# First recurrent head pair: its value projection spread over the parts of its triangular inverse, and its first factors made ahead of the last two receptance mixes

## The reference, cut to what matters

```python
Pm = Pf + (prev - Pf) * mu                    # token shift mix, Pf = u @ w_in
r, k, v = Pm[..., :C], Pm[..., C:2*C], Pm[..., 2*C:3*C]
kk = normalise(k * k_k);  k = k * (1 + (a - 1) * k_a)
...
def _wkv_step(S, inp):
    r_t, w_t, k_t, v_t, a_t, b_t = inp        # a_t = -kk, b_t = kk * a
    sa = einsum('bhvk,bhk->bhv', S, a_t)
    S = S * w_t + sa * b_t + v_t * k_t        # outer products
    y = einsum('bhvk,bhk->bhv', S, r_t)
```

## Time and profile before

| | |
|---|---|
| time, median of 3 runs | 1675.3 us (1672.17 to 1677.74) |
| profiled execution | 1668.06 us, its span 1666.3 us |
| mean granted TensorE clock | 0.977 of 2.4 GHz |
| PE, PEld, DVE, ACT busy | 93%, 63%, 41%, 26% of the span |
| stretch of this change | about 90 to 148 us from the span's start |

### The profile page before, as it was taken

How to read it: one execution, slowest core, us unless ns; L and a number is a source line. 1 busy time by engine, 2 the same in 40 slices (tenths; PEclk the granted TensorE clock), 3 DMA queues, 4 the chain that set the end, 5 groups by cost and what they waited for, 6 DMA issues and landing times. The chain is left out here.

```text
span 1666.3 us, 34650 instructions
## 1 busy us (share of the span) xinstructions
PE 1546.1 (93%) x14946; PEld 1056.2 (63%) x14946; DVE 683.7 (41%) x1685; ACT 425.3 (26%) x876; POOL 54.7 (3%) x57
## 2 busy tenths in 40 slices
PE   7998999999999998998989989999999999995997
PEld 4566676776767656675667664555686777672442
DVE  4455375466455324425152343224552111112564
ACT  4411413413421312405132241113111111111444
POOL 0000000000000000000000000000101010102110
PEclk9899999999999999999999999999999999997999
DMA  5000000100010106504343285004599999995321
GB/s 195 29 28 3 26 17 16 41 16 16 16 42 10 41 10 249 243 14 178 127 191 128 88 313 197 26 38 177 196 380 346 383 382 366 386 386 193 101 89 45
DMA packets 55614, 238.52 MB, mean 143 GB/s; under 512 B 7584, under 2 KB 18080, under 8 KB 45728
## 3 DMA queue, kind: packets, MB, share of 16 engines
q1 hardware_dynamic: 45776, 201.63, 31.8%
q0 software_dynamic: 6176, 22.02, 4.2%
q10 hardware_dynamic: 3504, 12.58, 1.9%
HBM read 206.53 MB, written 29.69 MB: 142 GB/s over the span
## 5 line engine op out<-in xcount | busy, mean ns | idle before, releaser
L465 PE MATMUL bank<-h,w 128*128 128x352 f32 (+1 forms) x528 | 182.2, 492 | 0.0
L465 PEld LDWEIGHTS bank<-h,w 128*128 128x128 f32 x528 | 99.6, 198 | 54.9 <-issue 6.1
L1950 PEld LDWEIGHTS bank<-cache,we 128*128 128x128 f32 x1088 | 123.4, 192 | 11.8 <-issue 7.2
L1950 PE MATMUL bank<-cache,we 128*128 128x96 f32 (+1 forms) x1088 | 124.7, 275 | 3.4 <-DVE cache L2281 3.4
L2281 DVE COPY cache<-bank 128x512 f32<-128x512 f32 (+1 forms) x54 | 31.6, 626 | 218.0 <-PE bank L1929 217.7
L2559 PE MATMUL bank<-we,unT 128*128 128x512 f32 x256 | 113.3, 601 | 1.4 <-DVE unT L2510 1.4
L1872 PE MATMUL bank<-cache,mixed 128*128 128x512 f32 x256 | 114.2, 606 | 0.0
L1362 PE MATMUL bank<-h,w 128*128 128x352 f32 (+1 forms) x288 | 88.4, 469 | 0.0
L1872 PEld LDWEIGHTS bank<-cache,mixed 128*128 128x128 f32 x256 | 49.2, 194 | 59.7 <-issue 59.7
L2559 PEld LDWEIGHTS bank<-we,unT 128*128 128x128 f32 x256 | 48.7, 193 | 59.8 <-issue 58.0
L1972 PE MATMUL bank<-we,gated 128*96 128x512 f32 (+2 forms) x192 | 79.5, 595 | 0.0
(11 more groups left out here) (432 smaller groups left out, 2622.5 us busy)
## 6 DMA issues: line engine op xcount, KB each, us to landing
we<-in_weg SPq DMA_DIRECT2D x24, 1024.0 KB
we<-in_weu SPq DMA_DIRECT2D x24, 1024.0 KB
we<-in_wed SPq DMA_DIRECT2D x24, 1024.0 KB
cache<-in_kcj SPq DMA_DIRECT2D x4, 5120.0 KB, 15.8
cache<-in_vcj SPq DMA_DIRECT2D x4, 5120.0 KB, 15.5
cache<-in_weg SPq DMA_DIRECT2D x8, 1024.0 KB, 15.5
cache<-in_weu SPq DMA_DIRECT2D x8, 1024.0 KB, 18.5
cache<-in_wed SPq DMA_DIRECT2D x8, 1024.0 KB
```

Source lines behind the costliest of these rows:

```text
L465: mm = pe.matmul(out[:, 0:w], w3[:, KIND[q], kd, :], g.uT[:, kd, a:a + w], start=(kd == 0), stop=(kd == KD - 1))
L1950: mm = pe.matmul(bank[6 + u % 2][:, 128 * (2 * a + f):128 * (2 * a + f) + CAPS[e]], weights[load_of[e] % NW][a][:, k, 128 * f:128 * f + 12 ...
```

## The change

1. v0 and v1 leave the end of `between(-1)`; v2 leaves its place ahead of part 0. All 24 matmuls of v0, v1 and v2 are issued one by one between the parts: one matmul, then two parts, four times; then one matmul and one part, twenty times. They go to banks 1, 2 and 0.
2. The products for j = 0 no longer wait for v.
3. On DVE the first factors of pair 0 are made before the mixes of r1 and r2, not after them (`factors`).
4. The DVE mixes of v0, v1 and v2 stand behind part 9, part 19 and part 27 of the inverse's answers.

Pairs 1 to 3 keep their order.

```diff
-                found += [("r", n, j + 1) for n in (1, 2)] + [("v", n, j + 1) for n in range(2)]
+                found += [("r", n, j + 1) for n in (1, 2)]
+                if j >= 0:
+                    found += [("v", n, j + 1) for n in range(2)]
...
-                        if ahead:
+                        if ahead and j >= 0:
                             job(j, "v", n // 2, halves[n % 2])
...
                     pe.wait_ge(s["r_ev"], 3 * j + 3)
-                    pe.wait_ge(s["v_ev"], 3 * j + 2)
+                    if j:
+                        pe.wait_ge(s["v_ev"], 3 * j + 2)
...
-                        project("v", 2, j, bank[0], range(KD))
+                        if j:
+                            project("v", 2, j, bank[0], range(KD))
                     if jp is None:
-                        parts(PARTS)
+                        pe.wait_ge(s["w3_v"], 16)
+                        for h in range(3 * KD):
+                            if h == KD:
+                                pe.wait_ge(s["b_init"], 2)
+                            project("v", h // KD, j, bank[(1, 2, 0)[h // KD]], (h % KD,))
+                            parts(1 + (h < PARTS - 3 * KD))
                         return
...
+                    def factors():
+                        dve.drain()
+                        dve.wait_ge(s["a_exp"], jn + 1)
+                        dve.scalar_tensor_tensor(out=ar[:, :, 0, :], in0=c3(kk[:, :]), scalar=-1.0, in1=c3(gain_before[:, :]), op0=ALU.mult, op1=ALU.mult)
+                        dve.tensor_tensor(bk[:, :, 0, :], c3(tmp[:, :]), c3(gain_inv[:, :]), ALU.mult).then_inc(s["a_k"], 1)
...
                         dve.tensor_tensor(tmp[:, :], kk[:, :], icl[:, :], ALU.mult)
+                        if not own:
+                            factors()
                         shift_in(jn, "r", 1)
...
-                        shift_in(jn, "v", 0)
-                        shift_in(jn, "v", 1)
+                        if own:
+                            shift_in(jn, "v", 0)
+                            shift_in(jn, "v", 1)
...
-                        shift_in(j, "v", 2).then_inc(s["a_v"], 1)
+                        if j:
+                            shift_in(j, "v", 2).then_inc(s["a_v"], 1)
                     if jp is None:
-                        parts(PARTS)
+                        for n in range(3):
+                            parts(10 if n < 2 else PARTS)
+                            end = shift_in(j, "v", n)
+                        end.then_inc(s["a_v"], 1)
                         return
```

More of the change, by code:

```diff
@@ L362, in jobs @@
             if after(j) is not None:
-                found += [("r", n, j + 1) for n in (1, 2)] + [("v", n, j + 1) for n in range(2)]
+                found += [("r", n, j + 1) for n in (1, 2)]
+                if j >= 0:
+                    found += [("v", n, j + 1) for n in range(2)]
             return found
-        job_bank = lambda j, q, n: n if (j, q) == (-1, "k") else next(4 + i % 3 for i, z in enumerate(jobs(j)) if z[:2] == (q, n))
+        job_bank = lambda j, q, n: n if (j, q) == (-1, "k") else (1, 2)[n] if (j, q) == (-1, "v") else next(4 + i % 3 for i, z in enumerate(jobs(j)) if z[:2] == (q, n))
         s = g.sems["rwkv"] | g.sems["early"]
```

## The result

The change makes the kernel slower: 1678.1 us (median of 20 runs) against 1670.5 us (20 runs), ratio 1.0046 with a 95% interval of 1.0030 to 1.0063, that is 5.0 to 10.5 us. The forecast was +5.5 us. Ratios leave out executions in which the chip was in its slower state (one of the 20 of the changed kernel, 1705.0 us at a granted clock of 0.929).

What follows compares the result with a forecast made beforehand. PE, busy 93% of the span, was taken as the bound. +4.6 us at the hand-over and 0.9 for the clock made +5.5, let through to the end: 1675.3 + 5.5 = 1680.8 us, range 1672.5 to 1687.

Steps and rivals of the forecast that it cites:

- Products earlier: Products ahead of the first inverse: they wait only for ACT's copy of r2 and start at 96.63, 9.35 us earlier.
- first_parts by DVE's own queue: DVE ahead of the inverse: first_parts starts at 101.7, held by DVE's queue and no longer by PE, 6.8 us earlier.
- Lost cover: PE under first_parts: some 5 us that v2 filled before are idle, with waits near 2.7 and 1.9 us.
- A single value matmul costs 0.93 us: PE inside the inverse: 0.14 us to get in plus 0.79 until the next tile, against 0.60 in a train.
- rival B: Inverse: value weights load under small tiles, a single costs the train's 0.60; hand-over -2.5 us, 1672.8 us; chance 0.15.
- DVE's mixes: Inverse and behind: v0's mix stalls PE 0.45 us at part 12; v1's costs nothing, v2's lies under pair 1's key projection.
- Clock: Thin PE stretch 101.8 to 107.1: half clock around 105 to 109 or 112, taken as 0.9 us, bounds 0 and +6.8.
- Hand-over: End of the inverse: DVE answers 0.77 us after part 27 starts, PE goes on 0.80 later, at 147.9, +4.6 us.
- Rival C: Inverse: half clock lasts longer or DVE's answers come late; +8 to +11.4 us, 1683.3 to 1686.7; chance 0.15.
- D: Behind the hand-over: the delay does not pass on; 0 to +1 us, 1675.3 to 1676.3; chance 0.10.

Runs made afterwards that it cites:

- v0_first: Changed kernel with DVE's v mixes after part 27, v0's eight matmuls ahead of part 0, sixteen singles ahead of parts 12 to 27: r2 to hand-over 53.7 us against 59.6.
- pairs: Changed kernel with DVE's v mixes after part 27 and the 24 value matmuls in 12 twos: r2's start to hand-over 55.6 us against 59.6.
- mixes_last: Changed kernel with DVE's mixes of v0, v1 and v2 all behind the answer to part 27: r2's start to hand-over 59.3 us against 59.6.

## Why the prediction was right

By its steps, in distances from r2's start (predicted, measured in the changed kernel):

- **Products earlier**: 6.63, 6.63 us. ACT's copy of r2 was the last thing waited for, as said.
- **first_parts by DVE's own queue**: 11.7, 11.67 us.
- **Lost cover**: part 0 at 14.5, part 1 at 17.1; measured 14.4 and 17.1, with two waits for L1188 of 2.59 and 1.93 us (2.7 and 1.9). v0_first shows that filling this stretch, with the entries it saves, gives 5.6 us back.
- **A single value matmul costs 0.93 us**: this decided the sign. Steps of z and x took 119.71 - 118.30 = 1.41 us (1.40), of t 121.58 - 119.71 = 1.87 (1.86), a level 9.39 (9.3). Part 8 to part 27 took 147.29 - 116.88 = 30.4 us, where 29.8 and the stall had been worked out: 30.25. pairs shows it from the other side: the second matmul of a two costs 0.59. From a value matmul to the small tiles behind it the weight loads do not run ahead. In the changed kernel's PEld timeline the engine is idle 0.49 us ahead of the tile loads that follow each value matmul, without a wait that the trace could name:

```profile
117.51 0.30 PEld L467 LDWEIGHTS bank<-h,w 128*128 128x128 f32 x2
118.30 0.56 PEld L712 LDWEIGHTS bank<-mixed,xb 64*64 64x64 f32 x32 [0.49 <-issue]
118.92 0.30 PEld L467 LDWEIGHTS bank<-h,w 128*128 128x128 f32 x2
119.71 1.01 PEld L714 LDWEIGHTS bank<-xb,mixed 64*64 64x64 f32 x32 [0.49 <-issue]
```

  So rival B is out here. The Trainium skill, page "TensorE: Matmul & The Clock Gate", part 3, says that weight loads overlap with matmuls in flight only where the row groups differ; a value matmul fills all row groups, and these rows agree with that. Inside a group of value matmuls they don't: in pairs a load of 128 x 128 weights begins at 121.03 us while the matmul row of 121.03 runs, with the same row groups, and nothing is lost. So that rule alone doesn't say where loads run ahead, and it is not shown as the cause of the 0.33 us. The semaphore wait that each part begins with isn't the cause either: in pairs the second z part of the row at 122.01 has one at 122.47, and the starts go on 15 ns apart. What the runs show is that the 0.33 us are paid once for each group of value matmuls: one takes 0.79 us to the next tile, two 1.38, four 116.65 - 114.09 = 2.56.
- **DVE's mixes**: the stall ahead of part 12 was 0.32 us in the trace and 0.3 in mixes_last (0.45 predicted); v1's and v2's cost nothing, nor did ACT's query copy and table load: the hand-over shift of 5.54 us is found again unchanged at L553, behind the key projection.
- **Clock**: the fall came in the predicted place and lasted to 112; this term was mis-sized. I had priced that case at up to 1.15 us and taken 0.9. Part 4 started at 23.0 us (112.20 - 89.22) instead of 21.35, and part 8 at 27.7 instead of 26.0, so it cost 1.6. The rows doubled nearly as assumed (a value matmul took 108.82 - 107.35 = 1.47 us to the next tile); what I had too large is how much of that the waits for DVE absorb. From part 1 to part 4 the prediction's own placing has 4.25 us, of which 0.75 and 0.23 are waits and 3.27 work, so doubled work could cost up to 3.27 - 0.98 = 2.3 us and not 1.15. Measured it was 112.20 - 106.29 = 5.91 us, with no wait left.
- **Hand-over**: 1.56 us after part 27 starts (1.57).

The sum was +5.5 and the stretch shows +6.3: 0.7 more for the clock, the rest roundings. Rival C did not come in the stretch itself. D is refuted by the shift that passes on undiminished. The forecast's other weak point was the level: the median of the three runs shown (1675.3) lay 5 us above that of twenty, so the forecast of 1680.8 stands 2.7 us above the 1678.1 measured though the difference was put 2 us too small: the two errors partly cancel, which is luck.

## What to carry to other kernels

Work put "between" the links of a chain is free only up to the waits that the chain really has: here 1.38 us a level, while six single matmuls brought 5.6. Price the switch as well as the work, from a place in the trace where the two kinds already alternate; with a fixed cost per switch, group to the size at which the chain's answers just keep up (twos here), and spend the rest first where another engine is busy anyway (DVE's first_parts). Before moving something earlier, look what it was hiding.

## What the runs showed of the hardware that was not expected

- A float32 128 x 128 matmul of 352 columns that stands alone between 64 x 64 tiles takes 0.79 us from its start to the next tile's, two take 1.38; to get in costs a further 0.14 to 0.16. In the earlier trace rows the same 0.79 was seen in quite another stage.
- Two t parts take 1.86 us from their first to their last start where two z parts take 0.94, though both are 32 matmuls of 64 x 64 (pairs, rows of 118.62 and 122.01): the 64 starts of L714 are 29.6 ns apart, those of L710 15.0. The kernel before shows the same at 126.49 and 115.70. z and x write to two banks by turns, and t to one, and t's tiles also come in another order; no run tells the two apart.
- In four of the kernels PE stood idle 0.27 to 0.55 us in the middle of a part with "issue" as the only reason, six times in all, always after 23 rows of the 32 of a part (in L709, L712 or L714); in the other six kernels, with the same instructions in another order, it did not do so in this stretch. Its cause stays open.
